# A hybrid attention layer: VectorE copies a sparse pair's transposed probabilities in front of scaling a finished head, not behind it

## The reference, cut to what matters

```python
s_s = jnp.einsum('bghqd,bgqkd->bghqk', qc, k_sel) * scale + bias_s
p_s, _ = masked_softmax(s_s, (dist_s >= 0)[:, :, None])
o_s = jnp.einsum('bghqk,bgqkd->bghqd', p_s.astype(dtype), v_sel)
...
p_w, _ = masked_softmax(s_w, band_w & (kpos >= 0)[None, :])
o_w = jnp.einsum('bghqk,bgkd->bghqd', p_w.astype(dtype), vwc)
return gc[..., 0:1] * o_c + gc[..., 1:2] * o_s + gc[..., 2:3] * o_w
```

## Time and profile before

| | |
|---|---|
| three runs | 1144.45, 1145.95, 1146.83 us |
| median | 1145.95 us |
| the profiled execution | 1146.21 us |
| its span, first to last instruction | 1144.3 us |
| granted TensorE clock, mean | 0.997 |
| busy: PE, DVE, ACT, POOL | 1131.5, 790.0, 551.6, 112.0 us |
| sparse stage, about | 590 to 633 us of the span |
| low copies (L1949) | 20, of 681 to 693 ns |
| scalings of a finished branch (L1987) | 8, of 691 to 692 ns |

### The profile page before, as it was taken

How to read it: one execution, slowest core, us unless ns; L and a number is a source line. 1 busy time by engine, 2 the same in 40 slices (tenths; PEclk the granted TensorE clock), 3 DMA queues, 4 the chain that set the end, 5 groups by cost and what they waited for, 6 DMA issues and landing times.

```text
span 1144.3 us, 18877 instructions
## 1 busy us (share of the span) xinstructions
PE 1131.5 (99%) x7148; PEld 991.7 (87%) x7148; DVE 790.0 (69%) x1208; ACT 551.6 (48%) x1008; POOL 112.0 (10%) x222
## 2 busy tenths in 40 slices
PE   9999999999999999999999999999999999999997
PEld 7889999988887888887977888887889999998886
DVE  5888888865356365444878553688689888888863
ACT  6245555542225312245778522357445555556543
POOL 0000000056006021000001400002000000000002
PEclk9999999999999999999999999999999999999999
DMA  7313333375954697454200223344223333336541
GB/s 222 106 53 100 110 110 110 111 257 199 379 221 151 209 333 226 128 168 146 78 2 2 76 74 110 129 163 132 74 78 101 91 100 110 110 113 212 203 154 73
DMA packets 148430, 157.99 MB, mean 138 GB/s; under 512 B 4868, under 2 KB 125868, under 8 KB 146812
## 3 DMA queue, kind: packets, MB, share of 16 engines
q1 hardware_dynamic: 139184, 117.46, 33.5%
q0 software_dynamic: 9072, 39.66, 9.6%
q10 hardware_dynamic: 112, 0.03, 0.0%
HBM read 140.10 MB, written 21.49 MB: 141 GB/s over the span
## 4 chain that ended last, share of the span: by engine, by line
PE 96%; DVE 1%; ACT 1%; issue 1%; DVEq 0%; POOL 0%; ACTq 0%; POOLq 0%
PE ps L2189 28%; PE ps L2296 28%; PE ps L2329 10%; PE ps L2355 7%; PE ps L2484 4%; PE ps L2802 3%; PE ps L2374 3%; PE ps L2780 2%; PE ps L2615 1%; PE ps L2639 1%; PE ps L2768 1%; PE ps L2546 1%; PE ps L2585 1%; PE ps L2567 1%; PE ps L2556 1%
## 5 line engine op out<-in xcount | busy, mean ns | idle before, releaser
L1436 DVE TENSOR_TENSOR ring_lo<-ring_raw,ring_hi 128x2048 fp32r<-128x2048 f32 (+1 forms) x56 | 126.5, 2261 | 114.5 <-ACT ring_hi L937 114.5
L937 ACT ACTIVATE ring_hi<-ring_raw 128x2048 fp32r<-128x2048 f32 (+1 forms) x56 | 105.3, 1883 | 188.4 <-PE ps L2329 71.0
L2189 PE MATMUL ps<-xn_hi,ring_hi 128*128 128x512 f32 x472 | 186.8, 396 | 2.7 <-DVE xn_lo L1475 2.3
L2189 PE MATMUL ps<-xn_hi,ring_lo 128*128 128x512 f32 x472 | 184.4, 391 | 0.0
L2189 PE MATMUL ps<-xn_lo,ring_hi 128*128 128x512 f32 x472 | 184.4, 391 | 0.0
L2296 PE MATMUL ps<-s_hi,ring_hi 128*128 128x256 f32 x512 | 145.0, 283 | 0.0
L2296 PE MATMUL ps<-s_hi,ring_lo 128*128 128x256 f32 x512 | 145.0, 283 | 0.0
L2296 PE MATMUL ps<-s_lo,ring_hi 128*128 128x256 f32 x512 | 145.0, 283 | 0.0
L2296 PE MATMUL ps<-x_hi,ring_hi 128*128 128x256 f32 x384 | 108.8, 283 | 0.0
L2296 PE MATMUL ps<-x_lo,ring_hi 128*128 128x256 f32 x384 | 108.7, 283 | 0.0
L2296 PE MATMUL ps<-x_hi,ring_lo 128*128 128x256 f32 x384 | 108.7, 283 | 0.0
(11 more groups left out here) (389 smaller groups left out, 2386.0 us busy)
## 6 DMA issues: line engine op xcount, KB each, us to landing
ring_raw<-in_ffn_w_gu SPq DMA_DIRECT2D x86, 512.0 KB, 4.9
ring_raw<-in_w_in SPq DMA_DIRECT2D x42, 512.0 KB, 4.9
ring_raw<-in_ffn_w_down SPq DMA_DIRECT2D x40, 512.0 KB, 4.4
ring_raw<-weight_sums SPq DMA_DIRECT2D x24, 512.0 KB, 4.3
down_block<-in_ffn_w_down POOLq DMA_DIRECT2D x8, 1024.0 KB, 9.3
weight_sums<-down_block POOLq DMA_DIRECT2D x8, 1024.0 KB, 9.4
out_block<-in_w_out POOLq DMA_DIRECT2D x4, 1024.0 KB, 9.0
weight_sums<-out_block POOLq DMA_DIRECT2D x4, 1024.0 KB, 11.5
```

Of the source, the lines that this page charges most:

```text
L937: e = act.activation(dst, src, ACT.Copy)
L1436: e = dve.tensor_tensor(dst, src, f32(r), ALU.subtract)
L2189: e = pe.matmul(ps[:, 2 * (slot if pair is None else pair) + c, :], part(a, slot, k * 256 + c * P, P), xn[b][:, k, :], start=(k == 0 and i ...
```

## The change

In DVE's loop over the pairs, the low copy of the pair before is issued ahead of the branch of a finished head. Nothing else differs.

```diff
@@ -2043,12 +2043,12 @@
                 if pair == NP + 3:
                     scale_gate(0)
                     lo(0, GATE + 2)
+                if P0 < pair <= NP:
+                    take_low_pT(pair - 1)
                 for b, done in ((0, S_DONE), (1, W_DONE)):
                     j, rest = divmod(pair - done - 4, 5)
                     if rest == 0 and 0 <= j < HPG:
                         take_branch(j, b)
-                if P0 < pair <= NP:
-                    take_low_pT(pair - 1)
                 for u in (2 * pair + 2, 2 * pair + 3):
                     if pair == P0:
                         cmp_out(u - 4 - NDU)
```

## The result

The kernel with the change takes 1.0030 of the time before, with a 95% interval of 1.0023 to 1.0038: 2.6 to 4.3 us more, 3.4 us at the ratio. Its fastest of 11 executions took 1147.20 us, the fastest of 11 before 1143.98 us, 3.2 us apart. The medians (1149.34 and 1144.45 us) lie 4.9 us apart, because executions of either kernel fall into two groups some 2 us apart: four of 11 fell into the upper one before the change, seven of 11 after it.

A forecast was written before the change was run, and what follows sets the result against it. TensorE's queue was taken to bound the kernel, VectorE's late biases reaching it through ScalarE. Five delays of 0.64 us, 3.2 us, on the median of 1145.95 gave 1149.15 us, range 1147.3 to 1150.9 us.

The forecast's parts named there:

- One branch, 0.64 us: VectorE, sparse stage: waiting for the copy's transposes before a finished head's branch starts the first bias 0.64 us later.
- both kinds: Finished-head branches due at S_DONE or W_DONE: each delays the first bias 0.64 us, totalling 1.9 and 1.3 us.
- No slack on the way: From VectorE's bias through ScalarE's exponentials and copy to TensorE: every link already waits, so all 0.64 us arrives.
- The two delays add: Within one head's cycle, the S_DONE and W_DONE delays of 0.64 us each add; 594.8 to 609.0 stretches from 14.2 to 15.5 us.
- The sixth: Last W_DONE branch, at 629 us: gate matmuls hide its delay with some 2 us over; uncovered, it would cost 0.64 us.
- What is earlier: The low copy starts 0.41 us earlier, but the next transposes needing its bank come 0.6 us after its old end: no gain.
- The later branch result: The branch's result comes 1.24 us later, covered by that turn's transposes and scores, so costed at nothing.
- The clock: TensorE, sparse stage: about 4.1 us of work in five keeps clock 1.00, nothing added; rival of falling clock, chance 0.07.
- the two rows: Profile rows before: 4.33 us of work at 475 us held clock 1.00; 3.65 us at 795 us was followed by 0.92, 0.73.
- Half of it: Rival, chance 0.13: only S_DONE or only W_DONE branches are paid, 1.9 or 1.3 us, giving 1147.9 or 1147.2 us.
- Nothing: Rival, chance 0.05: TensorE's later waits take the delay up, so the time stays at 1146.0 us.
- faster: Rival, chance 0.03: TensorE's transposes wait for the low copy, 0.41 us sooner in six places, 2.5 us saved, 1143.5 us.

The follow-up runs named there:

- the kernel that has it alone: Against the kernel before, low copy ahead of the branch only at pair 28; executed once, transposes to second gate step's turn back 45.85 us (45.86 before).
- The two extra instructions: Kernel before plus, in six turns, a VectorE addition or copy of bias-table rows between low copy and biases: 1.0066 and 1.0042; copy in branchless turns 0.9999.
- the kernel with the extra copy in the branch turns: Kernel before plus a VectorE copy of one bias-table row between low copy and biases in the six turns with a branch: 1.0042 of before.
- biases first but last: Against the kernel before, low copy, both biases, then branch in five turns, old order at pair 28; executed once, transposes to second gate step's turn back 46.12 us.
- w branches alone: Against the kernel before, low copy ahead of the branch only in the three turns where a W_DONE branch is due: 1.0015 of before.

## Why the prediction was right

It gave 1149.15 us against the median shown then, 3.2 us more, and a range of 1147.3 to 1150.9; slower by more than 0.2% with 0.76. Measured are 3.3 us in the stretch, 3.4 us by the ratio and 3.2 us between the fastest executions. That the forecast of 1149.15 lies 0.2 us from the median of 1149.34 is luck: the medians of 11 are 4.9 us apart, because with more executions the one before fell from 1145.95 to 1144.45, while the one after lies in the upper group.

- *What bounds.* Right: TensorE, and the waits that the change lengthens are the five that were there, with no new one.
- *One branch, 0.64 us.* Right for both kinds: 0.64 us from transposes to bias, and +0.65 us in each of three, +0.64 in each of two waits. The 0.75 us from transposes to a waiting copy held in front of a branch (594.11 to 594.86, 600.52 to 601.27).
- *No slack on the way.* Right, and shown three ways: with one kind at a time, and with two other sizes of delay.
- *The two delays add.* Right: 1.28 us for a cycle.
- *The sixth is covered.* Right, shown by the kernel that has it alone. The cover left over, 2.03 us of the predicted "some 2 us".
- *What is earlier gains nothing.* Right: no TensorE wait vanished.
- *The later branch result costs nothing.* Right for 1.24 us. The kernel with the biases ahead of the branch shows where this cover ends: a result that is 2.8 to 2.9 us later costs 0.27 us a place, and 1.03 us in the last turn, so the cover is some 2.5 us, and 1.9 us in the last turn.
- *The clock.* The estimate of 4.1 us of work in five microseconds was met (595 to 600 has 4.11, below) and the clock stayed at 1.00, as forecast. But the comparison with the two rows did not decide it: other profiles have the same 3.65 us of work at 795 to 800 us with the clock at 1.00 (last section). The swing of the clock that the Trainium skill describes (TensorE: Matmul & The Clock Gate, "A second HAM failure mode: psum-queue depth-cycling") did not appear in this stage, with TensorE waits of up to 0.90 us after the change.
- *The rivals.* Half of it: dead, both kinds are paid. Nothing, and faster: dead. One figure was on the low side: the scatter of a median was put at 0.5 us, while 11 executions of the changed kernel have a median 2.1 us above their fastest, and the median before moved by 1.5 us.
- *One sign did not come.* All that follows 633 us was to keep its length, and the span of the profiled execution was to be about 1147.5 us. It was 1145.3, since what follows became shorter, as told next.

In the profiled executions the spans differ by 1.0 us only (1144.3, 1145.3), less than the stretch. The parts: the stage began 0.68 us earlier in the one after (594.11 for 594.79), the stretch is 3.27 us longer, and what follows took 502.06 us for 503.65, 1.59 us less. The last is the clock, as far as the rows go: between the transposes of x (L2213) at 794.64 and at 808.47 us lie 13.83 us before, and 12.26 us after (797.19 to 809.45), which is 1.57 of the 1.59 us, and there the clock had fallen only before.

## What to carry to other kernels

Of two pieces of work that one engine takes in turn, the one whose input its producer makes first goes first. Put the other way round, an engine that gets there ahead of both inputs, as VectorE did here, idles for the time between them. What that idle costs is read from what stands behind it on the engine, here the biases, and from whether each link after it is already waiting. Here each link was: behind TensorE waits of 0.20 and 0.24 us, further delays of 0.64, 1.12 and 1.38 us were paid in full, and where a gate step stood in between, 0.64 us cost nothing. And before the order on a full engine is turned about, look for one that idles at that very place: moving six copies to ScalarE took 0.86 us off the stretch, while the orders on VectorE that had the copy in front in five or six places added 0.26 to 3.27 us.

## What was not expected

**VectorE beside GpSimd.** The two extra instructions, which read only SBUF, took much longer while GpSimd added (L887). Groups by line and form, the extra instructions in the branch turns and elsewhere; first the copy:

```profile
L2053 DVE COPY p_sb<-bias_n 128x512 f32<-128x512 f32 x6 | 7.1, 1190 | 0.0
```

```profile
L2053 DVE COPY p_sb<-bias_n 128x512 f32<-128x512 f32 x6 | 2.5, 418 | 0.0
```

and the addition of two rows, elsewhere (in the branch turns it is the row of 1.45 us above):

```profile
L2053 DVE TENSOR_TENSOR p_sb<-bias_n 128x512 f32<-128x512 f32 x6 | 4.1, 682 | 0.0
```

The timeline of the kernel with the extra copy in the branch turns, VectorE and GpSimd:

```profile
596.21 1.28 POOL L887 TENSOR_TENSOR y_nsa<-y_nsa,o_tmp 128x512 f32<-128x512 f32 x1 [27.90 <-DVE o_tmp L1987]
...
596.57 1.20 DVE L2053 COPY p_sb<-bias_n 128x512 f32<-128x512 f32 x1
```

The copy ends at 597.77, 0.28 us after GpSimd's addition (597.49), and 0.42 us is what it takes alone; it looks as if it waited for GpSimd to end rather than shared with it. The addition of two rows fits this: it ends at 597.39, 0.55 us after GpSimd's (595.57 + 1.27), and takes 0.68 us alone. Both ends lie 0.13 to 0.14 us short of a full run behind GpSimd's end, and both instructions took 0.77 us more although one is longer than the other. That reading is from the ends alone; no run moves GpSimd's start against VectorE's. Copies out of PSUM beside the same addition keep their 0.68 us. The biases, one input of which lies in PSUM, keep their 0.41 us (beside GpSimd's addition from 596.19 to 597.46 us). The Trainium skill (VectorE: DVE Perf Modes, "Two Vector instructions with no wait between them") names a second SBUF read interface, shared with GpSimd, that VectorE uses for the second of two SBUF inputs or in a mode with two ports. Both forms that were slow here would be such, if the copy runs in that mode, which no row names. That section gives no price; 0.77 us for each was the price in these places.

**TensorE's clock further on.** At the start of the second SwiGLU block the kernel before fell to granted 0.92 and 0.73; the profiled execution after did not, though TensorE was busy for 8.65 of the 10 us in both (with 42 matmuls before and 50 after):

```profile
795.00:800.00 5.00, 4.80 (x30) 3.59 (x28) 4.08 (x10) 2.23 (x9) 4.26 (x4) 1.00 0.00 0
800.00:805.00 5.00, 3.85 (x20) 3.03 (x20) 4.10 (x6) 4.78 (x6) 0.00 (x0) 1.00 0.00 0
```

The prediction priced such a dip at 1.75 us; what follows the stretch was 1.59 us shorter without it. The dip does not belong to the kernel before. Of the twelve kernels' profiles two have it, the one before and the one with biases first but last, both at 795 to 805 us; the other ten stand at 1.00 there. That kernel, and then the one with w branches alone, whose TensorE was as busy from 795 to 800 us and yet kept its clock:

```profile
795.00:800.00 5.00, 3.65 (x24) 2.54 (x23) 4.75 (x11) 3.31 (x8) 1.96 (x2) 0.97 0.00 0
800.00:805.00 5.00, 5.00 (x19) 3.96 (x18) 4.07 (x4) 3.21 (x4) 0.00 (x0) 0.69 0.00 0
```

```profile
795.00:800.00 5.00, 3.64 (x24) 2.53 (x23) 4.74 (x10) 2.89 (x7) 2.39 (x2) 1.00 0.00 0
800.00:805.00 5.00, 5.00 (x25) 4.08 (x24) 4.19 (x5) 3.58 (x4) 0.00 (x0) 1.00 0.00 0
```

Of the 11 executions of the changed kernel, the four of 1147.20 to 1148.10 us have a mean granted clock of 0.998 to 1.000, the seven of 1149.32 to 1149.68 us one of 0.997 to 0.998. So the same code at the same place gets the dip in some profiles and not in others. That it also makes the two groups of executions is likely from their clocks and from its size, but not shown: each kernel's clock was read by stretches in one execution only. Whether the change makes the upper group more frequent is open too; of the seven executions with the extra copy, whose waits are longer, all lie between 1149.71 and 1150.44 us with a mean clock of 0.999 to 1.000, which speaks against it. Inside the sparse stage, with its longer waits, the clock was at 1.00 from 590 to 640 us in the profile of every kernel of this study. From 590 to 640 us, five at a time, no window after the change has less work than this one:

```profile
595.00:600.00 5.00, 4.11 (x65) 3.16 (x64) 4.65 (x16) 3.76 (x14) 1.29 (x1) 1.00 0.01 3
```
